# A hybrid scan and expert-retrieval layer on one core: gates built over 64 blocks instead of 48, the projection in six token groups, V loads in another order

## The chip, the cores and the metric

The kernel runs on one core of one Trainium2 chip. The metric is the device time of an execution in microseconds, as the median of several runs; lower is better. Beside it there is one profiled execution, whose span (first to last instruction) and trace are read below.

## What is computed

One layer of a backbone over 1152 tokens (128 prompt tokens and 1024 latent ones) of width 1024: a modulated RMSNorm, an input projection, two kinds of chunked scans, an output projection, and then a product-key expert retrieval (PEER). Cut to the two parts that the change touches:

```python
proj = h @ w_in                          # (t, 1024) @ (1024, 3600)
z, xbc, dt_raw, rq, rk, rv, rg = split(proj)      # 512, 1024, 16, 512, 512, 512, 512
xbc = silu(depthwise_conv(xbc))
...
q = (h @ wq).reshape(t, 8, 2, 128)
s = einsum('thsd,hskd->thsk', q, keys)
s1, i1 = top_k(s[..., 0, :], 16); s2, i2 = top_k(s[..., 1, :], 16)
top, pos = top_k(s1[..., :, None] + s2[..., None, :], 16)
idx = i1 * 128 + i2 of pos; g = softmax(top)
act = gelu(einsum('tkd,td->tk', u_tab[idx], h))   # 128 of 16384 experts per token
y   = einsum('tk,tkd->td', g * act, v_tab[idx])
```

## The kernel before

The stages run one after another: modulation and norm, `project_in` (L291), the scans (`decay_terms`, `chunk_terms`, `mix_tokens`), `score_lists`, `hidden_and_gates` (L1443), `outputs` (L1774). A stage is a block in which every engine has its own stream, and the streams meet only in semaphores. All large products are made from two rounded halves of each operand, so each is three matmuls (`hi hi`, `hi lo`, `lo hi`); `hi` is a copy on ScalarE, `lo` a subtraction on VectorE or GpSimd.

**Projection** (`project_in`). First the 1024 columns of xbc, eight blocks of 128 columns, transposed (columns on partitions, tokens in three chunks of 384), each with a convolution on VectorE and a silu on ScalarE behind it. Then dt: for nine token tiles 24 matmuls of 16 columns each (L423). Then the other 2560 columns as five token groups of 512 columns, each nine tiles of 24 matmuls (L436); ScalarE copies a tile to `st` (L508), SP stores it. GpSimd loads the weights `wt` of group j+2 when group j is done; ScalarE splits them (`split_t`), VectorE makes the rest (`rest_t`, L525). Beside this VectorE makes 64 reductions for the modulation (L568), whose loads SP issues between the stores.

**U stage** (`hidden_and_gates`). The tokens are treated in two ways. Six tiles (768 tokens, TE) are dense: all 16384 experts are computed, as 128 blocks of 128 experts, `s = u h`, each block two halves of 24 matmuls with 384 columns (L1725), gelu on ScalarE (L1523) and a store to `s_d`. ScalarE splits a U block (L1518), GpSimd makes its low part (L1611, `low`) two blocks ahead. Three tiles (GT, 384 tokens) are gathered: GpSimd fetches 384 rows of U (one expert for each of 128 tokens, 512 KB, L1607) into rings of row buffers, and VectorE makes a dot product of each (L1632). In blocks 0 to H1 = 64, VectorE chooses the experts of the nine tiles (`choose`) with 144 (U1) dots between; when that is done it signals `sel_ready`, TensorE turns the lists, ScalarE copies them (`sel_copied`). In the gate blocks (H1 to H2 = 112) the dense gates are built: a group is 8 tokens; VectorE makes two one-hot arrays (L1691), ScalarE scales one by the gates (L1563, `put_gates`), TensorE multiplies them (L1741, `product`), ScalarE copies the result (L1556, `evacuate`) and after every fourth group sends 2 MB to `gates_d`. There are 96 groups, two per block, and 240 dots, five per block. A group needs the product two groups before it. When all dots are there, ScalarE makes their gelu and VectorE adds the first V1 = 48 rows of V.

**V stage** (`outputs`). 128 blocks of 128 experts in periods of BL = 4 blocks, buffers for eight blocks. For each block SP loads `vw` (512 KB) and `ga` (384 KB of `s_d`), and for each period `gt` (1.5 MB of gates). VectorE's `gated(e)` (L1895, 1897, 1899) multiplies by the gates and makes the low parts; ScalarE makes the high parts. TensorE has banks for three token tiles that are `kept` over the whole stage, and two for the other three, which are `taken` once per period: VectorE adds each to `acc` (`take`, L1910). A period on TensorE is taken(j,0), kept(j+1,0), taken(j,1), kept(j+1,1), taken(j,2), kept(j+1,2), kept(j+1,3): 24 matmuls of 512 columns (L1985) for each taken, 18 for each kept. `loads(j+2)` waits until taken(j,2) is done. GpSimd gathers the other VO = 336 rows of V (L1861) into eight buffers, and VectorE adds them (L1882) in `rows_between`, a share after each step of its stream; the shares end in period 27. `finish_first` completes the three gathered tiles, one after each take of period 29.

## Time and profile before

| | us |
|---|---|
| median of 3 runs | 3724.32 (3722.51 to 3728.41) |
| the profiled execution | 3714.26 |
| its span | 3712.6 |
| PE busy | 3380.9 (91%) |
| DVE busy | 2838.1 (76%) |
| POOL busy | 1754.5 (47%) |
| ACT busy | 1253.6 (34%) |
| DMA, mean over the span | 237 GB/s, 880 MB |

PE is TensorE's matmuls, PEld its weight loads, DVE VectorE, ACT ScalarE, POOL GpSimd, SP the engine that issues most loads and stores ("SPq" its queue). "L1725" is a line of the kernel. Times in a timeline are from the start of the span. "x24" is a count; what stands in square brackets at the end of a line is the idle time of the engine just before it and who ended it. PEclk is the granted clock of TensorE as a share of full speed; "DMA share" the mean busy share of the 16 DMA engines (the packets' own times can overlap, so it can pass 1). A matmul's end is modelled, so the pace of matmuls is read from start to start.

### The profile page before, as it was taken

What the parts mean: (1) busy time and instruction counts of PE and PEld (TensorE: products, weight loads), DVE (VectorE), ACT (ScalarE), POOL (GpSimd) and SP (SyncE); (2) the same over time, 40 slices, a digit from 0 to 9 for tenths busy, and PEclk for the clock granted to TensorE, in tenths of its full rate; (3) what the DMA queues carried; (4) which work ended last, traced back from release to release, by engine and by line L of the source; (5) the groups of instructions that cost most, each with busy time, mean ns of one, the idle gap of its engine ahead of it and who ended that gap; (6) DMA issues with size and microseconds to landing.
All of it is one profiled execution on the core that took longest, in us unless ns stands there. A gap on an engine that the chain in (4) does not pass through costs nothing. (4 is left out here: it accounts for less than half of the span.)

```text
span 3712.6 us, 50329 instructions
## 1 busy us (share of the span) xinstructions
PE 3380.9 (91%) x17854; PEld 2992.1 (81%) x17854; DVE 2838.1 (76%) x4693; ACT 1253.6 (34%) x2291; POOL 1754.5 (47%) x1014
## 2 busy tenths in 40 slices
PE   5999969599799999999898899996999999999998
PEld 2998859554799999999888888896777777778786
DVE  4544337497577899999899999954888888888887
ACT  2321125233323222222677777731212212212221
POOL 0000012121111487787788888874655565565530
PEclk8979979799899999999999999998999999999999
DMA  5225424542111578777889898887999999999993
GB/s 183 95 77 168 135 85 156 164 145 85 52 35 47 171 241 270 241 257 250 292 332 342 326 342 343 337 322 279 337 313 343 324 323 332 328 312 336 329 314 122
DMA packets 379343, 880.17 MB, mean 237 GB/s; under 512 B 33554, under 2 KB 192962, under 8 KB 376018
## 3 DMA queue, kind: packets, MB, share of 16 engines
q1 hardware_dynamic: 255876, 390.51, 32.4%
q0 software_dynamic: 116064, 423.24, 31.5%
q10 hardware_dynamic: 7280, 65.01, 4.5%
q8 instruction: 49, 0.80, 0.1%
q14 instruction: 74, 0.61, 0.1%
HBM read 740.54 MB, written 138.11 MB: 237 GB/s over the span
## 5 line engine op out<-in xcount | busy, mean ns | idle before, releaser
L1861 POOL DMA_INDIRECT hT<-peer_v,hT x336 | 571.5, 1701 | 450.9 <-DVE hrow L1882 367.8
L1725 PE MATMUL ps<-h_hi,u_hi 128*128 128x384 f32 x2048 | 699.9, 342 | 30.3 <-POOL u_lo L1611 22.5
L1725 PE MATMUL ps<-h_hi,u_lo 128*128 128x384 f32 x2048 | 690.2, 337 | 0.0
L1725 PE MATMUL ps<-h_lo,u_hi 128*128 128x384 f32 x2048 | 690.1, 337 | 0.0
L1985 PE MATMUL ps<-v_hi,a_hi 128*128 128x512 f32 x1536 | 607.0, 395 | 66.9 <-DVE acc L1910 36.2
L1985 PE MATMUL ps<-vw_rest,a_hi 128*128 128x512 f32 x1536 | 604.4, 393 | 0.0
L1985 PE MATMUL ps<-v_hi,ga_rest 128*128 128x512 f32 x1536 | 603.9, 393 | 0.0
L1607 POOL DMA_INDIRECT hT<-u_rows,hT x224 | 376.6, 1681 | 95.7 <-issue 51.6
L1882 DVE SCALAR_TENSOR_TENSOR hrow<-hT,dots,hrow 128x1024 f32<-128x1024 f32 x336 | 418.1, 1276 | 0.0
L1725 PEld LDWEIGHTS ps<-h_hi,u_hi 128*128 128x128 f32 x2048 | 389.6, 190 | 33.9 <-issue 29.6
L1611 POOL TENSOR_TENSOR u_lo<-uw,u_hi 128x1024 fp32r<-128x1024 f32 x126 | 340.1, 2699 | 157.8 <-ACT u_hi L1518 155.3
L1985 PEld LDWEIGHTS ps<-v_hi,a_hi 128*128 128x128 f32 x1536 | 292.1, 190 | 135.6 <-DVE acc L1910 43.8
L1725 PEld LDWEIGHTS ps<-h_lo,u_hi 128*128 128x128 f32 x2048 | 389.3, 190 | 0.0
L1725 PEld LDWEIGHTS ps<-h_hi,u_lo 128*128 128x128 f32 x2048 | 388.7, 190 | 0.0
L1985 PEld LDWEIGHTS ps<-v_hi,ga_rest 128*128 128x128 f32 x1536 | 292.3, 190 | 61.8
L1985 PEld LDWEIGHTS ps<-vw_rest,a_hi 128*128 128x128 f32 x1536 | 292.7, 191 | 60.9
L1632 DVE CUSTOM_DVE_ANT_0 hT<-hT,hrow 128x1024 f32<-128x1024 f32 x224 | 315.7, 1454 | 32.7 <-DMA hT<-u_rows,hT 31.5
L1523 ACT ACTIVATE so<-ps 128x384 f32<-128x384 f32 x256 | 123.7, 483 | 545.8 <-PE ps L1725 419.8
L1691 DVE TENSOR_TENSOR hT<-iota,sel 128x1024 f32<-128x1024 f32 x192 | 298.0, 1591 | 6.4 <-ACT sel L1546 6.4
L1563 ACT ACTIVATE hT<-hT,sel 128x128 f32<-128x128 f32 x768 | 235.5, 389 | 160.2 <-DVE hT L1691 160.2
L1607 POOL DMA_INDIRECT big<-u_rows,hT x160 | 268.3, 1677 | 43.8 <-issue 40.9
L1839 ACT ACTIVATE a_hi<-ga 128x768 fp32r<-128x768 f32 x128 | 108.5, 848 | 518.2 <-DVE ga L1895 518.2
(338 smaller groups left out, 5889.8 us busy)
## 6 DMA issues: line engine op xcount, KB each, us to landing
uw<-u_T SPq DMA_DIRECT2D x128, 512.0 KB
vw<-peer_v SPq DMA_DIRECT2D x128, 512.0 KB, 11.6
s_d<-so SPq DMA_DIRECT2D x256, 192.0 KB
gates_d<-big ACTq DMA_DIRECT2D x24, 2048.0 KB
gt<-gates_d SPq DMA_DIRECT2D x32, 1536.0 KB
ga<-s_d SPq DMA_DIRECT2D x128, 384.0 KB, 12.1
wmr<-w_modT SPq DMA_DIRECT2D x32, 512.0 KB
tok_d<-st SPq DMA_DIRECT2D x45, 256.0 KB, 2.2
```

The source lines that it names most:

```text
L1523: act.activation(so[b][:], g.ps[4 + 2 * s + b][:, 0:HALF], ACT.Gelu_apprx_tanh).then_inc(act_done, 1)
L1563: z = act.activation(one[s][:, q], one[s][:, q], ACT.Identity, scale=sel3[:, 2, r * G + q:r * G + q + 1])
L1607: pool.indirect_dma_start(rows[slot], None, table, bass.IndirectOffsetOnAxis(ap=g.pick[q][:, i:i + 1], axis=0)).then_inc(row_loaded[slot], 16)
L1611: pool.tensor_tensor(u_lo[e % 2][:], uw[e % 2][:], f(u_hi[e % 2][:]), ALU.subtract).then_inc(u_lo_ready, 1)
L1632: z = dve.tensor_tensor_reduce(rows[slot], rows[slot], g.hrow[:, n // NSEL], 1.0, 0.0, ALU.mult, ALU.add, g.dots[:, n // NSEL, n % NSEL:n ...
L1691: z = dve.tensor_tensor(hot, numbers, sel3[:, i, r * G:(r + 1) * G].unsqueeze(2).broadcast_to([P, G, P]), ALU.is_equal)
L1725: mm = pe.matmul(g.ps[4 + 2 * s + b][:, 0:HALF], u[s][:, k, :], h[:, k, b * HALF:(b + 1) * HALF], start=(k == 0 and i == 0), stop=(k == KD ...
L1839: act.activation(a_hi[s][:], a[s][:], ACT.Copy).then_inc(a_hi_ready, 1)
L1861: pool.indirect_dma_start(rows[n % NU], None, g.v_rows, bass.IndirectOffsetOnAxis(ap=g.pick[m % GT][:, m // GT:m // GT + 1], axis=0)).then ...
L1882: dve.scalar_tensor_tensor(g.hrow[:, q], rows[n % NU], g.dots[:, q, i:i + 1], g.hrow[:, q], ALU.mult, ALU.add).then_inc(added, 1)
L1985: mm = pe.matmul(bank[:], aa[s][:, t * P:(t + 1) * P], v[s][:, q * 512:(q + 1) * 512], start=(start and i == 0), stop=(stop and i == 2), s ...
```

## The change

Three things are changed.

- Projection: dt has no matmuls of its own any more. Its 16 columns stand behind the others, and 16 columns of zeros behind them, in a table `w_tok` of 2592 columns, made on the host; six groups of TW = 432 columns take the place of five of 512. xbc has its own table `w_xbc`. ScalarE copies the first three tiles of the first group ahead of the last silu.
- U stage: the gate blocks are 60 to 123 (64 of them, `PAIRS` = 32 pairs). The first three of the four halves of a pair have a group each. U1 is 128, so 128 dots lie among the lists and 256 in the gate blocks, eight per pair. V1 is 12. ScalarE's loop from H1 on is written out.
- V stage: SP issues the second period's loads only when the second `vw` has landed, and GpSimd its first gather when five blocks are gated. The 372 rows are spread over 29 periods, in shares of 2, 3, 5 and 2 steps; gated() of a period's first block stands behind the five, that of its second behind take(j+1,0), the third and fourth behind take(j+1,1). The three `finish_first` follow one another after the last take of period 29.

```diff
-TC = PROJ - XBC
+TW = 432
+TC = 6 * TW
...
             body(0, 0)
-            with eng.Fori(0, 2) as i:
+            body(1, 1)
+            with eng.Fori(1, NG // 2) as i:
+                body(i * 2, 0)
                 body(i * 2 + 1, 1)
-                body(i * 2 + 2, 0)
...
-            pool.dma_start(wd[:], wv[:, :, 512 + XBC:REST0]).then_inc(wd_loaded, 16)
-            pool.dma_start(wt[0][:], wv[:, :, 0:512]).then_inc(wt_loaded[0], 16)
-            pool.dma_start(wt[1][:], wv[:, :, REST0:REST0 + 512]).then_inc(wt_loaded[1], 16)
+                pool.dma_start(wx[s][:], wv[:, :, s * P:(s + 1) * P]).then_inc(wx_loaded[s], 16)
+            for j in range(2):
+                pool.dma_start(wt[j][:], tv[:, :, j * TW:(j + 1) * TW]).then_inc(wt_loaded[j], 16)
...
-            for j in range(3):
-                pool.wait_ge(group_done, j + 1)
-                c = REST0 + (j + 1) * 512
-                pool.dma_start(wt[j % 2][:], wv[:, :, c:c + 512]).then_inc(wt_loaded[j % 2], 16)
+                    pool.dma_start(wx[s][:], wv[:, :, bass.ds(i * (2 * P) + (2 + s) * P, P)]).then_inc(wx_loaded[s], 16)
+            for j in range(2, NG):
+                pool.wait_ge(group_done, j - 1)
+                pool.dma_start(wt[j % 2][:], tv[:, :, j * TW:(j + 1) * TW]).then_inc(wt_loaded[j % 2], 16)
...
-            pe.wait_ge(wd_lo_ready, 1)
-            for t in range(NT):
-                rows = slice(t * P, (t + 1) * P)
-                for k in range(KD):
-                    for m, (h, w) in enumerate(((h_hi, wd_hi), (h_hi, wd_lo), (g.hT_lo, wd_hi))):
-                        mm = pe.matmul(g.ps[6][:, 16 * t:16 * t + 16], h[:, k, rows], w[:, k, :],
-                                       start=(k == 0 and m == 0), stop=(k == KD - 1 and m == 2))
-            mm.then_inc(dt_done, 1)
-            pe.wait_ge(banks_free, NB + 2)
+            pe.wait_ge(banks_free, NB + 1)
...
-                            mm = pe.matmul(g.ps[t % NQ][:], h[:, k, rows], w[s][:, k, :],
+                            mm = pe.matmul(g.ps[t % NQ][:, 0:TW], h[:, k, rows], w[s][:, k, :],
...
             split_t(1)
+
+            def group(grp, tiles):
+                for t in tiles:
+                    act.wait_ge(tile_done, grp * NT + t + 1)
+                    act.wait_ge(st_stored[t % NQ], grp * (16 * NT // NQ) + (t // NQ) * 16 + 16)
+                    act.activation(st[t % NQ][:], g.ps[t % NQ][:, 0:TW], ACT.Copy).then_inc(tile_copied, 1)
+            group(0, range(NQ))
             silu(NB - 1, 1, NB // 2 - 1)
             act.wait_ge(mod_small, 64)
             act.activation(cb2[:], cb2[:], ACT.Silu).then_inc(mod_silu, 1)
-            act.wait_ge(dt_done, 1)
-            act.activation(dts[:], g.ps[6][:, 0:16 * NT].rearrange("p (t c) -> p t c", t=NT), ACT.Copy).then_inc(dt_copied, 1)
-
-            def group(grp, s):
-                for t in range(NT):
-                    act.wait_ge(tile_done, grp * NT + t + 1)
-                    act.wait_ge(st_stored[t % NQ], grp * (16 * NT // NQ) + (t // NQ) * 16 + 16)
-                    act.activation(st[t % NQ][:], g.ps[t % NQ][:], ACT.Copy).then_inc(tile_copied, 1)
-            for grp in range(5):
-                group(grp, grp % 2)
-                if grp < 3:
+            for grp in range(NG):
+                group(grp, range(NQ if grp == 0 else 0, NT))
+                if grp + 2 < NG:
...
-H1, BODY = 64, 8
-H2 = H1 + DENSE * BODY
+H1 = 60
+H2 = H1 + 64
 NU = 8
 RING1, RING2 = 8, 12
-U1 = 144
+U1 = 128
 LEAD = 8
-V1 = 48
+V1 = 12
...
+            def store_gates(c):
+
+                act.wait_ge(copied, 8 * (c + 1) + 2 * R)
+                act.dma_start(g.gates_d[c].rearrange("p b t -> p (b t)"), out[c % 2]).then_inc(g_stored[c % 2], 16)
...
+            for e in range(H1, NE):
+                for b in range(2):
+                    i = (e - H1) % 2 * 2 + b
+                    if e < H2 and i < THREE:
+                        r = (e - H1) // 2 * THREE + i
+                        evacuate(r)
+                    gelu_half(e, e % 2, b)
+                    if e < H2 and i < THREE and r % 4 == 3:
+                        store_gates(r // 4)
+                if e + 2 < NE:
+                    split_u(e + 2, e % 2, (e + 2) // 2)
+                if e == H2:
+                    act.wait_ge(dots_done, GT * NSEL)
+                    act.activation(g.dots, g.dots, ACT.Gelu_apprx_tanh).then_inc(gelu_done, 1)
...
-            for d in range(DENSE):
-                for k in range(BODY):
-                    e = H1 + d * BODY + k
-                    many = u_rows_by(e) - u_rows_by(e - 1)
-                    group(d * PER + 2 * k)
-                    n = dots(n, many // 2)
-                    group(d * PER + 2 * k + 1)
-                    n = dots(n, many - many // 2)
+            for p in range(PAIRS):
+                many = u_rows_by(H1 + 2 * p + 1) - u_rows_by(H1 + 2 * p - 1)
+                for i in range(THREE):
+                    group(p * THREE + i)
+                    n = dots(n, many * (i + 1) // THREE - many * i // THREE)
...
-            with pe.Fori(0, DENSE) as d:
-                for k in range(BODY):
-                    e, s = d * BODY + (H1 + k), k % 2
+            with pe.Fori(0, PAIRS // 2) as m:
+                for k in range(4):
                     for b in range(2):
-                        product(d, 2 * k + b)
-                        half(e, s, b)
+                        i = k % 2 * 2 + b
+                        if i < THREE:
+                            product(m * (2 * THREE) + (k // 2 * THREE + i), k // 2 * THREE + i)
+                        half(m * 4 + (H1 + k), k % 2, b)
...
-STEPS = 6 + 7 * 28
+SHARE = (2, 3, 5, 2)
+STEPS = sum(SHARE) * 29
...
-            for j in range(2):
-                gates(j, j)
-                loads(j, j)
+            gates(0, 0)
+            loads(0, 0)
+            sp.wait_ge(v_loaded[1], 16)
+            gates(1, 1)
+            loads(1, 1)
...
-            for s in range(RING - 2):
+            for s in range(RING - 3):
                 ready(NE - RING + s, s, NE // RING - 1)
             root(0)
-            for s in range(RING - 2, RING):
+            for s in range(RING - 3, RING):
...
+            pool.wait_ge(a_ready, BL + 1)
...
-            def rows_between(step):
-
-                for n in range(min(VO * step // STEPS, VO), min(VO * (step + 1) // STEPS, VO)):
+            def rows_between(step, many):
+
+                for n in range(min(VO * step // STEPS, VO), min(VO * (step + many) // STEPS, VO)):
                     add_row(n)
-                return step + 1
+                return step + many
...
-            for e in range(BL + 2):
+            for e in range(BL + 1):
                 gated(e)
-                step = rows_between(step)
-            for j in range(NB - 2):
+            for j in range(NB - 1):
                 for t in range(TR):
                     take(j, t)
-                    if j == NB - 3:
-                        finish_first(t)
-                    step = rows_between(step)
-                    for e in ((BL * (j + 1) + 2 + t,) if t < 2 else (BL * (j + 2), BL * (j + 2) + 1)):
-                        gated(e)
-                        step = rows_between(step)
-            dve.sem_inc(ms_ready, 1)
-            for t in range(TR):
-                take(NB - 2, t)
-                if t < 2:
-                    gated(NE - 2 + t)
+                    if j == NB - 3 and t == TR - 1:
+                        for q in range(GT):
+                            finish_first(q)
+                    for e in ((1,), (2, 3), ())[t]:
+                        gated(BL * (j + 1) + e)
+                    step = rows_between(step, SHARE[t])
+                if j < NB - 2:
+                    gated(BL * (j + 2))
+                    step = rows_between(step, SHARE[3])
+                if j == NB - 3:
+                    dve.sem_inc(ms_ready, 1)
...
-        "w_in": A["w_in"][0],
+        "w_xbc": f(A["w_in"][0][:, 512:512 + XBC]),
+        "w_tok": f(np.concatenate([A["w_in"][0][:, 0:512], A["w_in"][0][:, REST0:], A["w_in"][0][:, 512 + XBC:REST0],
+                                   np.zeros((D, TC - (PROJ - XBC)), np.float32)], 1)),
```

## Rows read from the trace of the kernel before

**Rows 1.** Windows: busy us of each engine in two stretches of 100 us (columns named).

```profile
core 0: us, PE busy (x) PEld busy (x) DVE busy (x) ACT busy (x) POOL busy (x), PEclk, DMA share, GB/s
2000.00:2100.00 100.00, 89.77 (x586) 86.80 (x585) 92.03 (x102) 75.11 (x170) 82.53 (x45) 1.00 0.92 346
3000.00:3100.00 100.00, 96.30 (x416) 78.94 (x416) 83.62 (x86) 20.74 (x23) 58.75 (x35) 0.98 0.95 326
```

**Rows 2.** The chain that ended last, V stage: start us, us, what.

```profile
2709.60 7.07 DMA ga<-s_d
...
2743.87 11.73 DMA ga<-s_d
...
3527.25 159.48 PE ps L1985 x702
```

**Rows 3.** Matmuls of the projection by line: min/median/max ns, first and last start us.

```profile
L423 PE MATMUL ps<-wdt_hi,pi_h_hi x72: 171/361/362, 196.7 to 238.2; 128*128 128x16 f32 x72
...
L436 PE MATMUL ps<-wt_hi,pi_h_hi x360: 388/394/774, 238.8 to 490.0; 128*128 128x512 f32 x180
```

**Rows 4.** Timeline before the token groups, ACT, then DVE: start us, us, instruction.

```profile
194.67 3.61 ACT L458 ACTIVATE wt_hi<-wt 128x4096 fp32r<-128x4096 f32 x1
...
198.31 4.42 DVE L525 TENSOR_TENSOR wt_rest<-wt,wt_hi 128x4096 fp32r<-128x4096 f32 x1 [3.22 <-ACT wt_hi L458]
```

**Rows 5.** Timeline of ACT, first halves of two plain blocks of U.

```profile
2505.57 0.49 ACT L1523 ACTIVATE so<-ps 128x384 f32<-128x384 f32 x1 [3.57 <-PE ps L1725]
...
2513.89 0.49 ACT L1523 ACTIVATE so<-ps 128x384 f32<-128x384 f32 x1 [3.58 <-PE ps L1725]
```

**Rows 6.** Timeline where the gate blocks begin, DVE, then ACT.

```profile
1762.16 1.21 DVE L1632 CUSTOM_DVE_ANT_0 hT<-hT,hrow 128x1024 f32<-128x1024 f32 x1
1763.31 0.07 DVE L1632 DVE_READ_ACCUMULATOR2_ANT dots<- 128x1 f32 x1
...
1768.41 0.50 DVE L1679 COPY hT<-big 128x128 f32<-128x128 f32 x3
...
1771.58 0.49 ACT L1523 ACTIVATE so<-ps 128x384 f32<-128x384 f32 x1 [3.67 <-PE ps L1725]
...
1794.26 0.47 ACT L1523 ACTIVATE so<-ps 128x384 f32<-128x384 f32 x1
```

**Rows 7.** Groups of instructions by form in the gate blocks, 1850 to 2400 us.

```profile
L1691 DVE TENSOR_TENSOR hT<-iota,sel 128x1024 f32<-128x1024 f32 x163 | 257.4, 1618 | 0.0
L1607 POOL DMA_INDIRECT big<-u_rows,hT x133 | 226.4, 1702 | 36.4 <-issue 34.3
...
L1632 DVE CUSTOM_DVE_ANT_0 big<-big,hrow 128x1024 f32<-128x1024 f32 x135 | 178.5, 1349 | 21.3 <-DMA big<-u_rows,hT 21.1
...
L1611 POOL TENSOR_TENSOR u_lo<-uw,u_hi 128x1024 fp32r<-128x1024 f32 x41 | 112.5, 2745 | 40.2 <-ACT u_hi L1518 39.9
```

**Rows 8.** Timeline of gate blocks: a product on PE, then first halves on ACT.

```profile
1934.16 2.05 PE L1741 MATMUL ps<-hT 128*128 128x128 f32 x16
...
2427.32 0.53 ACT L1523 ACTIVATE so<-ps 128x384 f32<-128x384 f32 x1
```

**Rows 9.** Timeline at the start of the V stage, SP queue and PE.

```profile
2568.35 9.43 SPq L1814 DMA_DIRECT2D vw<-peer_v  x1
...
2594.43 0.77 PE L1985 MATMUL ps<-v_hi,a_hi 128*128 128x512 f32 x1 [30.65 <-DVE ga_rest L1899]
```

**Rows 10.** One V period on DVE, then a stall on PE: timeline.

```profile
3309.10 0.96 DVE L1895 TENSOR_TENSOR ga<-ga,gt 128x768 f32<-128x768 f32 x1 [6.98 <-DMA ga<-s_d]
...
3311.98 2.47 DVE L1882 SCALAR_TENSOR_TENSOR hrow<-hT,dots,hrow 128x1024 f32<-128x1024 f32 x2
...
3005.89 0.50 PE L1985 MATMUL ps<-v_hi,a_hi 128*128 128x512 f32 x1 [2.95 <-DVE acc L1910]
```

**Rows 11.** Row gathers of the V stage by line: first and last start us.

```profile
L1861 POOL DMA_INDIRECT hT<-peer_v,hT x336: 939/1696/4626, 2568.6 to 3569.4; - x168
```

**Rows 12.** Window of 10 us near the start of the V stage; columns as in rows 1.

```profile
2610.00:2620.00 10.00, 10.00 (x46) 8.29 (x45) 10.00 (x12) 3.60 (x4) 8.69 (x4) 1.00 1.04 394
```

More of the change, by code:

```diff
@@ L299, in project_in @@
     NQ = 3
+    NG = TC // TW
     with ExitStack() as ctx:
@@ L431, in group @@
                     rows = slice(t * P, (t + 1) * P)
-                    if not (isinstance(grp, int) and t < NQ):
+                    if not (isinstance(grp, int) and grp * NT + t < NQ):
                         pe.wait_ge(tile_copied, grp * NT + (t - NQ + 1))
@@ L1566, in _ @@
             put_gates(1, 1)
-            for d in range(DENSE):
-                for k in range(BODY):
-                    e, s = d * BODY + (H1 + k), k % 2
-                    for b in range(2):
-                        q = 2 * k + b
-                        evacuate(d, q)
-                        if d * PER + q + R < TE // G:
-                            put_gates(d * PER + q + R, q % R)
-                        gelu_half(e, s, b)
-                    split_u(e + 2, s, d * (BODY // 2) + (H1 + k) // 2 + 1)
-                    if k % 2 == 1:
-                        act.wait_ge(copied, d * (2 * PER) + 4 * (k + 1) + 2 * R)
-                        act.dma_start(g.gates_d[bass.ds(d * 4 + k // 2, 1)].rearrange("o p b t -> p (o b t)"), out[k // 2 % 2]).then_inc(g_stored[k // 2 % 2], 16)
-            plain(H2, 0, H2 // 2)
-            act.wait_ge(dots_done, GT * NSEL)
-            act.activation(g.dots, g.dots, ACT.Gelu_apprx_tanh).then_inc(gelu_done, 1)
-            plain(H2 + 1, 1, H2 // 2)
-            with act.Fori(H2 // 2 + 1, NE // 2 - 1) as j:
-                plain(j * 2, 0, j)
-                plain(j * 2 + 1, 1, j)
-            gelu(NE - 2, 0)
-            gelu(NE - 1, 1)
+            for e in range(H1, NE):
[12 more added lines that the diff above has]
+                    act.activation(g.dots, g.dots, ACT.Gelu_apprx_tanh).then_inc(gelu_done, 1)
             for s in range(2):
@@ L1731, in hidden, with product @@
                 half(e, s, 1, first)
-            def product(d, q):
-                r = d * PER + q
+            def product(r, q):
                 pe.wait_ge(hot_ready, r * 2 + 2)
```

54 lines of the change are left out of this document (20 added, 34 removed).

## Prediction

> **What bounds the kernel now.** I read the windows by stage first, then the chain that ended last, then for each stage the group or the timeline that shows which wait ends last. The profiled execution spans 3712.6 us (3714.26 us with what lies around it); the median of the runs shown is 3724.32, so 10 us above it. I sum against 3714.26 and add the 10 at the end. Three stages are touched. (1) The projection: TensorE is busy without a break, but part of that is 216 tiny matmuls for dt [rows 3]. (2) The U stage (128 blocks of 48 matmuls): a plain block takes 8.32 us, from first half to first half [rows 5]. In the 48 gate blocks VectorE is 92% busy, TensorE 90%, GpSimd 83% and the DMA engines 92% [rows 1]; from the first half of block 64 (1794.26) to that of block 111 (2427.32) it is 47 blocks in 633 us, 13.5 each [rows 6, 8]. (3) The V stage: TensorE 96%, DMA 95%, VectorE 84% [rows 1]; the chain goes in turn through a load landing, VectorE, TensorE [rows 2]. So here the order of VectorE's work against the landing decides, with the DMA engines close behind.
>
> **Projection, part by part.** Removed: 216 dt matmuls, which run from 196.7 to 238.8 [rows 3]: 42.1 us on TensorE with nothing beside them that needs the time. Added: 16 columns of dt and 16 of padding in the token groups. Before: 45 tiles of 24 matmuls with 512 columns in 251 us (238.8 to 490.0), 5.58 per tile, 232 ns per matmul; the plain pace is 227 ns at 512 columns (159.48 us / 702, [rows 2]) and 8.32 us / 48 = 173 ns at 384 [rows 5]. Between them, 432 columns give 193 ns, 54 tiles x 24 x 193 = 250.5 us; with six group ends instead of five and the slow first matmuls (774 ns against a median of 394, [rows 3]) I take 255, so +4. The dt matmuls also covered the split of the first weights: with them gone TensorE waits from 196.7 until wt_lo is there. Today ScalarE takes 3.61 us and VectorE then 4.42, until 202.7 [rows 4]; at 432/512 of that, and without the wdt split ahead, 201.2, so +4.5. Sum: -42.1 + 4 + 4.5 = **-34** (bounds -38 if the start costs nothing more, -28 if each group end waits 1 us for its weights or a store). ScalarE takes the first three tiles ahead of the last silu, so the fourth tile finds its bank free, and each later load of weights has most of a group's 42 us to land and be split.
>
> **Where the gate blocks begin.** VectorE finishes the lists and the gates at about 1768.9 (the copies that start at 1768.41, [rows 6]), TensorE the last half of block 63 at 1771.6, when ScalarE takes it. The two are level now. The change takes away four blocks (33.3 us) from TensorE but only 16 dots from VectorE, at 1.15 us (1762.16 to 1763.31, [rows 6]): 18.4 us. So TensorE will wait for sel_ready, and the gate blocks begin 18.4 us, not 33 us, earlier (bounds -15 and -22: the row gathers hold low parts of U a little more or less). The transposes and the first product cost the same as now: first half of block 64 at 1794.26 [rows 6], of block 60 then at 1776, before the 34 of the projection are taken off.
>
> **The gate blocks.** Per two blocks now: VectorE 8 comparisons x 1.618 + 10 dots x 1.349 = 26.4 us, GpSimd 2 x 2.745 + 10 gathers x (1.702 + 0.27 of issue) = 25.2 and a 2 us wait for u_hi [rows 7], TensorE 2 x 8.32 + 4 products of 1.8 = 23.8 (a product of 16 passes shows 2.05 with its modelled end [rows 8]; start to start it is 1.8). Measured 2 x 13.5 = 27, so VectorE and GpSimd set it. After: six comparisons and eight dots, 20.5 us on VectorE; 5.5 + 8 x 1.97 = 21.3 on GpSimd; 16.6 + 3 x 1.8 = 22.0 on TensorE, which becomes the bound. With three engines within 1.5 us of one another I don't take 22.0 but 23.2 (end points 22.0, and 25.0 if two of the waits stay as they are). 32 pairs x 23.2 = 742 us, to 2518; four plain blocks and the last two halves, 33 us, to 2551. The stage ends now at 2567.9, just ahead of the first issue of the next one [rows 9]. So the U stage gives **-17** with its start included (bounds -55 with pairs of 22.0, +41 with pairs of 25.0). The store of gates, 24 of 2 MB as before, and the wait for the gelu of the dots with 12 V rows behind it (12 x 1.3 = 16 us on VectorE) are hidden by the last three blocks (25 us).
>
> **The V stage.** 36 rows move here: 336 gathers from 2568.6 to 3569.4 now [rows 11], 372 after, spread over 29 periods instead of 28.
> - Start. TensorE begins at 2594.43, 26.5 us after the first load; the first weight load is stuck behind gt for 9.43 us in SP's queue [rows 9], while 8 row gathers and the second gt share the engines. With both held back, gt, one vw and one ga are 2.5 MB; at 394 GB/s [rows 12] 6.3 us, plus issue and landing and VectorE's 2.9, some 15 us: **-11** (bounds -5 and -15).
> - Periods. 144 matmuls at 227 ns are 32.7 us of TensorE. From the first kept blocks (2611) to the last row it is 28 periods in 974 us, 34.8 each. The 2.1 us are lost so: loads(j+2) are issued when taken(j,2) is done, land 7.1 to 11.7 us later [rows 2], and VectorE, which goes straight into gated() of the first two of these blocks, stands still (6.98 us in [rows 10]) and is then late for take(j+1,0), so TensorE waits 2.95 us for acc [rows 10]. The new order puts five row additions (1.2 us each, [rows 10]: 2.47 for two) ahead of one gated() (2.9 us) and the other gated() behind take(j+1,0): 9.4 + 2.9 + 2 rows x 1.2 + 0.6 = 15.3 us after taken(j,2), where TensorE wants take(j+1,0) after 17.7 us (kept 4.1 + 4.1, taken 5.4, kept 4.1). By this the stall is gone. Against it stands DMA: a period moves 5.24 MB of blocks and 12.8 rows of 0.52 MB, 11.97 MB against 11.53 now; at 32.7 us that is 366 GB/s, where the stage runs at 326 with the engines 95% busy [rows 1]. 10 us at 394 GB/s are seen [rows 12], so 366 is not out of reach, but not with loads that come in bursts. I take 34.7 us (345 GB/s, the value of [rows 1] for the gate blocks, 346). 29 x 34.7 = 1006, against 28 x 34.8 + 32.7 = 1007: **-1** (bounds 33.2 and 36.5 per period: -44 and +51).
> - End. The three finish_first now stand in one lump (some 11 us of VectorE) ahead of gated(124): TensorE reaches it after 13.6 us, VectorE after 14 or 15: **+3**.
>
> The Trainium skill, "DMA: Bandwidth & Descriptors", section Bandwidth, gives about 358 GB/s as a core's share of HBM, and 425 for a core alone. By 358 the period would be 33.4 us and the change worth 38 us more; the trace shows 394 for 10 us, above the share, and no long stretch above 346, so neither figure bounds the sum.
>
> **Sum**: -34 - 17 - 11 - 1 + 3 = -60; 3714.3 - 60 = 3654 for a profiled run, **3664 us** for the median.
>
> **Rivals.**
> - Forecast, 3664 us: chance 0.55.
> - V stage at TensorE's pace: nothing but the order held it, period 33.2. 29 x 1.5 = 43 less, 3621. For it: the stall row and its releaser. Against: 95% DMA. Chance 0.15.
> - V stage DMA-bound at today's rate: 11.97 MB at 331 GB/s (11.53 MB in 34.8) is 36.1 us; 29 x 1.4 = 41 more: 3705. For it: the engines 95% busy, and five gathers in a burst. Against: the stage loses that share partly in the stall. Chance 0.19.
> - Gate blocks stay late: GpSimd's gathers and low parts run into each other, 25.0 per pair, 32 x 1.8 = 58 more: 3722, no change that can be told (0.2% is 7 us, about what this measurement can tell). Chance 0.05.
> - Slower: the five row additions free five buffers just when loads(j+2) are issued, so five gathers compete with the first vw and ga. A row takes 1.5 us of all engines at 346 GB/s; three more than now ahead of the loads add 4.5 us, and equal shares with the rest of gt 2 more: landing at 16 instead of 9.4. Then gated() ends at 18.9, 5.3 us after TensorE wants it (13.6), and every period is 38: 29 x 3.3 = 96 more, 3760. It turns to slower than before once landings exceed 14.8 us (period 36.8). Against: the queue holds at most eight rows at any time now too. Chance 0.06.
>
> The Trainium skill, the same page, section Queues, rings and completion order, says that an engine takes turns between the queues it has work for, packet by packet. By this rule the loads would get about half of the engines while rows are queued, which is that last rival; 9.43 us for an issue behind gt [rows 9] speak for it, and no row shows the shares themselves.
>
> **Range**: 3622 to 3712 leaves out the slow rivals and half of the fastest one. Faster by over 0.2% 0.89, within 0.2% 0.05, slower 0.06.
>
> **What the profile would show.** No matmul of 16 columns, the token groups beginning near 201 and ending near 457. Block 60's half waiting for sel_ready, with VectorE the releaser. Gate pairs of 23.2 us, TensorE over 94% and VectorE under 92% busy. In V: first matmul 15 us after the stage begins, DVE's wait for ga short, no acc releaser on TensorE, DMA share 0.97 or more, period 34.7. The forecast fails if a gate pair takes 25 us, or if landing takes over 15 us in V.

## The result and the profile after

| | before | after |
|---|---|---|
| median, 4 runs each on one chip | 3725.64 us (3722.51 to 3728.41) | 3615.95 us (3615.19 to 3617.31) |
| ratio, 95% interval | | 0.9706 [0.9691, 0.9722] |
| span of the profiled execution | 3712.6 us | 3613.5 us |

The change saves 110 us where 60 were forecast, and the time lies below the range. Between the two profiled executions it is 99.1 us. Most of the other 11 are the distance of before's profiled execution from its own median: the runs of before lie between 3712 and 3733 us in all comparisons below, those of after within 2.1 us of one another.

By stage, worked out from the first and last instructions in the two traces (us):

| | before | after | change | forecast |
|---|---|---|---|---|
| start to the first U matmul | 1201.7 | 1180.3 | -21.4 | -34 |
| first U matmul to the first load of gt, where V begins | 1366.2 | 1351.4 | -14.9 | -17 |
| load of gt to the first V matmul | 26.5 | 15.9 | -10.6 | -11 |
| V matmuls, first to last (periods and end) | 1102.8 | 1050.6 | -52.2 | -1 + 3 |
| last V matmul to the end | 15.4 | 15.3 | 0 | 0 |

The V matmuls took 54 us less than forecast and the projection 13 us more; the other rows come within 2 us, the U stage by luck, as shown below. Windows of after, columns as in [rows 1]; two stretches of gate blocks, two of V:

```profile
2000.00:2100.00 100.00, 95.09 (x610) 94.08 (x609) 81.62 (x91) 68.37 (x147) 77.76 (x43) 0.98 0.88 320
2100.00:2200.00 100.00, 92.21 (x586) 90.90 (x586) 83.14 (x95) 68.57 (x153) 77.44 (x43) 0.98 0.88 320
3000.00:3100.00 100.00, 100.00 (x443) 82.84 (x442) 93.54 (x95) 21.93 (x24) 60.22 (x39) 1.00 1.00 365
3100.00:3200.00 100.00, 100.00 (x443) 82.84 (x442) 93.06 (x94) 21.91 (x24) 56.06 (x40) 1.00 1.02 370
```

In V TensorE has no gap left, where [rows 1] has 96%. VectorE is at 93%, since it adds more rows in a shorter time, and the DMA engines move 365 to 370 GB/s where it was 326. The chain that ended last says it in one row (start us, us, what):

```profile
2532.10 5.87 SPq L1792
2538.02 6.45 DMA ga<-s_d
...
2547.60 989.66 PE ps L1965 x4356
```

4356 of the 4608 matmuls follow one another without a wait, at 227.2 ns; 4608 of them are 1046.9 us, and they take 1050.6. In [rows 2] the chain came back to a landing of 7 to 12 us. The waits of VectorE in the V stage follow (total us, times, longest). The first pair of rows is before from 2600 to 3600; the second is after from 2560 to 3530, where these two rows are all there are:

```profile
DVE ga L1895 <- DMA ga<-s_d: 140.4, 36, 7.3
...
DVE acc L1910 <- PE ps L1985: 13.5, 10, 1.8
```

```profile
DVE acc L1891 <- PE ps L1965: 59.9, 35, 2.2
DVE acc L1888 <- PE ps L1965: 12.0, 4, 7.1
```

No wait for a load is left; VectorE waits for TensorE. A piece of one period of VectorE in after's timeline:

```profile
3016.67 1.28 DVE L1891 TENSOR_TENSOR acc<-acc,ps 128x512 f32<-128x512 f32 x2
3017.86 6.16 DVE L1863 SCALAR_TENSOR_TENSOR hrow<-hT,dots,hrow 128x1024 f32<-128x1024 f32 x5
3023.94 0.94 DVE L1876 TENSOR_TENSOR ga<-ga,gt 128x768 f32<-128x768 f32 x1
```

The next loads are issued when TensorE has done the bank that the first line of this piece adds to acc. VectorE adds five rows of V, 6.2 us, and then finds ga landed: there is no idle time in front of the third line, where [rows 10] has 6.98 us.

Part of the 52 us is TensorE's clock, which the forecast did not look at. The clock is granted at one of two levels, 1.2 or 2.4 GHz (PEclk 0.5 or 1.0). Behind the stall of 2.95 us in [rows 10] it stood at the lower one:

```profile
3007.00:3010.00 3.00, 3.00 (x8) 2.35 (x8) 3.00 (x4) 1.47 (x2) 2.69 (x2) 0.50 1.09 369
```

Matmuls start 0.43 us apart there (3006.69 to 3009.67) instead of 0.227. Over the V stage of before, 104 matmuls start 240 to 520 ns after the one ahead of them, together 18 us above the plain pace; in after it is 11, for 2 us. So about 16 of the 52 us are the lower clock that came with the stalls, and the rest is the stalls themselves.

### The profile page after: what moved, and what is told of

The parts are those of the page before. It is cut to its first block and busy times, and to the rows that moved or that the text cites. A ratio compares the mean times of both kernels' runs of the same rounds, so it can differ in the third digit from the quotient of the medians.

```text
span 3613.5 us, 50302 instructions
## 1 busy us (share of the span) xinstructions
PE 3330.6 (92%) x17854; PEld 2994.0 (83%) x17854; DVE 2813.8 (78%) x4693; ACT 1252.5 (35%) x2299; POOL 1653.7 (46%) x1014
## 5 line engine op out<-in xcount | busy, mean ns | idle before, releaser
L1842 POOL DMA_INDIRECT hT<-peer_v,hT x372 | 547.2, 1471 | 444.7 <-DVE hrow L1863 329.4
L1965 PE MATMUL ps<-v_hi,a_hi 128*128 128x512 f32 x1536 | 598.7, 390 | 22.9 <-DVE ga_rest L1880 20.4
L1863 DVE SCALAR_TENSOR_TENSOR hrow<-hT,dots,hrow 128x1024 f32<-128x1024 f32 x372 | 457.3, 1285 | 0.0
L1587 POOL DMA_INDIRECT hT<-u_rows,hT x212 | 342.6, 1616 | 120.5 <-DVE dots L1612 71.0
L1612 DVE CUSTOM_DVE_ANT_0 hT<-hT,hrow 128x1024 f32<-128x1024 f32 x212 | 296.4, 1441 | 60.0 <-DMA hT<-u_rows,hT 58.8
L1612 DVE CUSTOM_DVE_ANT_0 big<-big,hrow 128x1024 f32<-128x1024 f32 x172 | 225.1, 1339 | 100.1 <-DMA big<-u_rows,hT 100.0
L1587 POOL DMA_INDIRECT big<-u_rows,hT x172 | 276.8, 1609 | 46.5 <-issue 43.9
```

The lines of the kernel that those rows point to most:

```text
L1587: pool.indirect_dma_start(rows[slot], None, table, bass.IndirectOffsetOnAxis(ap=g.pick[q][:, i:i + 1], axis=0)).then_inc(row_loaded[slot], 16)
L1612: z = dve.tensor_tensor_reduce(rows[slot], rows[slot], g.hrow[:, n // NSEL], 1.0, 0.0, ALU.mult, ALU.add, g.dots[:, n // NSEL, n % NSEL:n ...
L1842: pool.indirect_dma_start(rows[n % NU], None, g.v_rows, bass.IndirectOffsetOnAxis(ap=g.pick[m % GT][:, m // GT:m // GT + 1], axis=0)).then ...
L1863: dve.scalar_tensor_tensor(g.hrow[:, q], rows[n % NU], g.dots[:, q, i:i + 1], g.hrow[:, q], ALU.mult, ALU.add).then_inc(added, 1)
L1965: mm = pe.matmul(bank[:], aa[s][:, t * P:(t + 1) * P], v[s][:, q * 512:(q + 1) * 512], start=(start and i == 0), stop=(stop and i == 2), s ...
```

## The experiments

The kernel before was run beside each group of them on the same chip; its medians were 3720.73, 3721.07 and 3719.86 us. All ratios are to these.

### Is V short by its own order, or by what comes before it?

**v_only** is before with the new V stage alone (336 rows in it); **v_old** is after with the whole V stage of before (372 rows).

```diff
 v_only: before, with outputs() and STEPS of after
 v_old:  after, with outputs() and STEPS of before
```

> The kernel of before with nothing changed but the V stage (new order and start; 336 rows as before). The order theory: TensorE's pace of 32.6 us per period, stage 1082 us as in the changed kernel, since rows are not what bounds it: 3725.6 - 63 = 3663 us. The rival, that 36 fewer rows in the U stage or the new gate blocks are needed for the gain: 3700 us or more.

> The changed kernel with the whole V stage of before (order of gated, takes and row additions, loads, start), but with the 372 rows. The order theory: VectorE stands still at the first ga of a period as before and has 36 rows more to add at 1.2 us, so the V stage (first gt issue to the end) takes 1144.7 + 43 = 1188 us instead of 1082, and the kernel 3722 us. The rival, that the V stage got shorter because of the U stage's end or the gates and not of its own order: V stage 1145 at most, 3680 us or less.

v_only took 3653.83 us (3648.03 to 3657.28), ratio 0.9824 [0.9804, 0.9844], near the 3663 of the theory of the order and far from the rival's 3700; v_old 3665.55 us (3650.94 to 3671.17), 0.9845 [0.9813, 0.9877]. From the load of gt to the end v_only needs 1081.8 us, as after does, against 1144.7 in before. Its windows show TensorE full:

```profile
2700.00:2800.00 100.00, 100.00 (x443) 82.81 (x442) 89.01 (x91) 21.90 (x24) 48.12 (x36) 1.00 0.95 344
3000.00:3100.00 100.00, 100.00 (x443) 82.81 (x442) 88.94 (x90) 22.04 (x24) 47.58 (x35) 1.00 0.96 350
```

So the gain of V belongs to the V stage alone, and a DMA share of 0.95 goes with a full TensorE, while the same share went with 96% in [rows 1]: the share alone did not tell whether the loads were the bound. v_old was 56 us faster than its expectation by the theory of the order (3722), which had 36 more rows lengthen every period. The V matmuls did not get longer: 1090.7 us in v_old against 1102.8 in before, with the DMA engines at 350 GB/s:

```profile
3100.00:3200.00 100.00, 96.21 (x424) 79.00 (x422) 88.10 (x90) 22.58 (x24) 63.32 (x38) 1.00 0.97 350
```

The reading that fits is that VectorE adds the extra rows in time in which it waited for ga: without the one long wait at the start of the stage it waits 102 us in v_old and 146 in before (134.5 - 32.4 and 182.3 - 36.2), and 36 rows at 1.2 us are 43. Why V then took 12 us less is open: V in the old order took 1102.8, 1111.5 and 1116.3 us in three kernels with identical V stages.

### The order undone, the rest left

**v_gated_first** is after with one thing put back: gated() of the next period's first block comes ahead of the five row additions. Rows, shares and start are those of after.

```diff
+                    if t == TR - 1 and j < NB - 2:
+                        gated(BL * (j + 2))
                     step = rows_between(step, SHARE[t])
                 if j < NB - 2:
-                    gated(BL * (j + 2))
                     step = rows_between(step, SHARE[3])
```

> The changed kernel with gated() of the next period's first block ahead of the five row additions instead of behind them. If the five rows that fill the landing time are what removed the stall: 9.4 + 2.9 + 7 x 1.2 + 0.6 = 21.3 us after taken(j,2), where TensorE wants take at 17.7, so 3.6 us per period and more with slow matmuls behind it: 3616 + 29 x 4 = 3732 us. The rival, that it is enough to have one gated() instead of two ahead of the take: 3616 to 3630 us.

Measured: 3709.21 us (3705.49 to 3715.8), ratio 0.9969 [0.9957, 0.9981]. The V matmuls take 1145.3 us, 94.7 more than in after, 3.3 a period. The same three instructions in its timeline, in the other order, and the wait that it makes; then the waits from 2560 to 3640 and two windows:

```profile
3124.84 1.28 DVE L1891 TENSOR_TENSOR acc<-acc,ps 128x512 f32<-128x512 f32 x2
3130.37 0.96 DVE L1876 TENSOR_TENSOR ga<-ga,gt 128x768 f32<-128x768 f32 x1 [4.25 <-DMA ga<-s_d]
...
3133.26 7.36 DVE L1863 SCALAR_TENSOR_TENSOR hrow<-hT,dots,hrow 128x1024 f32<-128x1024 f32 x6
```

```profile
DVE ga L1876 <- DMA ga<-s_d: 140.0, 29, 6.7
...
PE ps L1966 <- DVE acc L1891: 63.7, 29, 4.6
```

```profile
3000.00:3100.00 100.00, 96.87 (x417) 79.39 (x418) 85.89 (x89) 22.25 (x24) 58.12 (x34) 0.98 0.94 341
3100.00:3200.00 100.00, 90.77 (x379) 73.79 (x378) 87.08 (x88) 19.27 (x21) 51.02 (x39) 0.95 0.87 314
```

This is the cause, moved by hand: one instruction group in another place costs 93 us, and the rival (one gated() less ahead of the take is enough, 3616 to 3630) is out. The 93 us are the price of this place in the new schedule. They are not what before lost: after with the whole old V stage (v_old) is only 50 us slower than after, so v_gated_first is worse than the old order, and it waits more for ga (4.8 us a period, v_old 3.5). Why the old order waits less was not looked into. A ledger of VectorE gives the size of the 93. In after it is busy 827 of the 880 us from 2620 to 3500, 30.7 us of a period of 32.7. If it also waits 140.0 / 29 = 4.8 us in each, it needs 35.5, and TensorE must follow; the period measured is 36.0. The clock has a share in that: here 145 matmuls start 240 to 520 ns after the one ahead, together 25 us above the plain pace, so some 23 of the 94.7 us are the lower clock. Without the wait 30.7 is less than 32.7, and TensorE sets the pace. In before it is busy 843.5 us and waits 140.4 of the 1000 from 2600 to 3600, together 98% of the time: there too the two fill it.

### How much room did the DMA engines have?

**dma1** and **dma3** are after with one or three copies of 512 KB from HBM to HBM in each V period, which nothing waits for.

```diff
                     loads(m * 2 + i, i)
+                    for c in range(3):    # dma1: range(1)
+                        sp.dma_start(g.dump[...], g.u_rows[...]).then_inc(dumped, 16)
```

> The changed kernel with one more transfer per period of the V stage, 512 KB from one place in HBM to another, which nothing waits for until the end. At TensorE's pace the stage then moves 12.5 MB per period, 382 GB/s. The theory that DMA has no room left at 366 GB/s (engines at 1.00): periods of 12.5 / 366 = 34.2 us, 29 x 1.5 = 44 more, 3660 us. The order theory with room left up to the 394 GB/s seen for 10 us: 3616 to 3622 us.

> The kernel after with three more copies of 512 KB from HBM to HBM in each V period, which nothing else waits for: at 32.7 us a period that asks for 414 GB/s, where one copy (381 GB/s) cost nothing. If the ceiling of the DMA engines lies near the 394 GB/s of the window of the prediction, the period becomes 34.3 us and 29 x 1.6 = 46 us come on top: about 3662. If it lies at 381, the period is 35.5 us: about 3698. If 414 can still be had: 3616 to 3622.

dma1 took 3619.38 us (3617.9 to 3620.87), ratio 0.9724 [0.9709, 0.9739], with 1050.2 us of V matmuls; dma3 3716.14 us (3711.07 to 3729.99), ratio 0.9996 [0.9984, 1.0008], with 1151.4. Two windows of dma1, then one of dma3, and a piece of dma3's chain:

```profile
2700.00:2800.00 100.00, 100.00 (x443) 82.81 (x442) 94.69 (x96) 22.38 (x25) 58.94 (x42) 1.00 1.05 386
3000.00:3100.00 100.00, 100.00 (x443) 82.80 (x442) 93.53 (x95) 21.92 (x24) 58.24 (x40) 1.00 1.04 381
```

```profile
2800.00:3000.00 200.00, 189.58 (x826) 155.83 (x825) 173.96 (x175) 42.20 (x46) 109.64 (x73) 0.98 1.01 378
```

```profile
3088.80 17.58 DMA ga<-s_d
3109.51 53.82 PE ps L1968 x228
...
3165.19 10.89 DMA ga<-s_d
```

381 to 386 GB/s can be had without a matmul being late. With three copies, which ask for 414, the landings in the chain are 9 to 18 us, VectorE waits for ga again (89.7 us in 15 times from 2700 to 3600), and the period is 36.0 us (1050.6 + 100.8, the 100.8 spread over 30 periods), in which 13.54 MB move, 376 GB/s. That is worse than each of the three expectations; 3698 was the nearest. The rate alone would have given 13.54 / 0.386 = 35.1 us. Of the 100.8 us about 20 are matmuls at the lower clock (125 of them, counted as above, 22 us against 2 in after). What else makes up the rest, the rate of such copies or the burst in which they stand in the queue, wasn't separated, so 376 is no ceiling. For after it is enough: it asks for 366 GB/s and had 15 to 20 more.

The Trainium skill, "DMA: Bandwidth & Descriptors", section Bandwidth, has about 358 GB/s as a core's share when both cores of a pair stream, and 425 for a core alone. The traces agree in that a core alone moved 365 to 386 GB/s, above the share, in windows of 100 us; no run here reached 425, and where 414 was asked for, 376 came.

### The start of V by itself

**v_old_start** is after with the second gt and the row gathers no longer held back.

```diff
-            gates(0, 0)
-            loads(0, 0)
-            sp.wait_ge(v_loaded[1], 16)
-            gates(1, 1)
-            loads(1, 1)
+            for j in range(2):
+                gates(j, j)
+                loads(j, j)
...
-            pool.wait_ge(a_ready, BL + 1)
```

> The changed kernel with the old start of the V stage (both periods' loads at once, gathers at once). If the start is worth what the traces show, first matmul 26.5 us after the first issue instead of 16, and as the rest runs at TensorE's pace nothing of it is caught up: 3626.5 us. The rival, that the start is made up later: 3616 us. Its row shares begin at take(0,0) in either case.

Measured: 3630.04 us (3629.13 to 3630.97), ratio 0.9756 [0.9737, 0.9775]. The first V matmul comes 27.2 us after gt instead of 15.9, and the first weight load is stuck for 10.64 us again, where after has 5.87:

```profile
2534.47 10.64 SPq L1792 DMA_DIRECT2D vw<-peer_v  x1
```

The start is worth 11 us as forecast; the whole run is 14 us slower than after.

### The projection by itself

**proj_only** is before with the new project_in() and the weights laid out for it; **store_first** is after with each load of the modulation's weights issued four tiles later, behind the stores of the tiles.

```diff
 store_first:
-                    if 2 <= grp * NT + t < 4 * KD:
-                        load_mod(grp * NT + t)
                     sp.wait_ge(tile_copied, grp * NT + t + 1)
                     sp.dma_start(g.tok_d[...], st[t % NQ][:]).then_inc(st_stored[t % NQ], 16)
+                    if 2 <= grp * NT + t - 4 < 4 * KD:
+                        load_mod(grp * NT + t - 4)
```

> The kernel of before with the new projection alone. If the stages are independent, it gives what the two traces show up to the first matmul of U (1201.7 against 1180.3): 21 us less, 3699 us. My forecast of 34 us would give 3687 us. A rival, that the later stages answer to the shift: any other value, up to 3721.

> The changed kernel; in the projection SP stores a tile first and issues the modulation load of four tiles earlier after it, so that a store never waits behind a load that waits for VectorE. If the 12 us that TensorE stands still in the token groups come from that queue (st waits for a store, the store stands behind load_mod), the groups take 253 us instead of 264.6 and the kernel 3606 us. The rival, that they come from the first wait for weights and the group ends: 3616 us.

proj_only took 3696.85 us (3695.25 to 3701.38), ratio 0.9935 [0.9921, 0.9949]: 24 us, near the 21 of the two traces and not the 34 of the forecast. Its first U matmul is at 1174.6, 27 us earlier than in before. store_first took 3617.89 us (3614.96 to 3619.71), 0.9723 [0.9708, 0.9738]: nothing, as the rival had it. The token matmuls of after by line, TensorE's waits in 190 to 470 us, and ScalarE's wait for a free store buffer, in after and then in store_first:

```profile
L423 PE MATMUL ps<-wt_hi,pi_h_hi x432: 352/358/698, 204.0 to 468.2; 128*128 128x432 f32 x144
...
PE ps L423 <- ACT st L488: 4.8, 3, 3.5
PE ps L423 <- DVE wt_rest L509: 4.6, 1, 4.6
...
ACT st L488 <- DMA tok_d<-st: 61.3, 15, 9.8
```

```profile
ACT st L488 <- DMA tok_d<-st: 6.1, 1, 6.1
```

The groups take 264.6 us in after (before: 251.7) and 263.4 in store_first. ScalarE's 55 us of waiting for the store's queue vanish and TensorE gains 1 us. So hardly any of that wait reached TensorE, which has three banks between itself and ScalarE.

### Why a pair of gate blocks takes 24 us, not 22

The pairs of after are bound by no engine: in the windows at the top TensorE has 92 to 95%, VectorE 82%, GpSimd 78%. The pairs are not alike either. From the first matmul of a pair to that of the next, 15 pairs of after, from block 74 on, go 26.0, 23.7, 23.8, 22.0, 26.5, 23.0, 23.9, 22.0, 26.7, 22.8, 23.8, 22.0, 26.8, 22.8, 23.8 us: one in four is long, and one in four has the 22.0 that the work of TensorE adds up to. VectorE's waits from 1750 to 2300 follow, and one place in the timelines of VectorE, ScalarE and GpSimd, each in order of time:

```profile
DVE big L1612 <- DMA big<-u_rows,hT: 64.9, 30, 6.3
DVE hT L1612 <- DMA hT<-u_rows,hT: 36.2, 17, 7.0
```

```profile
1837.51 1.23 DVE L1612 CUSTOM_DVE_ANT_0 big<-big,hrow 128x1024 f32<-128x1024 f32 x1 [6.16 <-DMA big<-u_rows,hT]
...
1844.37 2.35 DVE L1671 TENSOR_TENSOR hT<-iota,sel 128x1024 f32<-128x1024 f32 x2
...
1848.93 4.56 DVE L1671 TENSOR_TENSOR hT<-iota,sel 128x1024 f32<-128x1024 f32 x2
...
1839.91 2.44 ACT L1551 ACTIVATE hT<-hT,sel 128x128 f32<-128x128 f32 x8 [7.11 <-DVE hT L1671]
...
1833.72 0.94 POOL L1587 DMA_INDIRECT big<-u_rows,hT  x1 [0.30 <-issue]
1834.68 2.36 POOL L1591 TENSOR_TENSOR u_lo<-uw,u_hi 128x1024 fp32r<-128x1024 f32 x1
...
1842.13 1.98 POOL L1587 DMA_INDIRECT big<-u_rows,hT  x1 [0.30 <-issue]
1849.49 2.92 POOL L1591 TENSOR_TENSOR u_lo<-uw,u_hi 128x1024 fp32r<-128x1024 f32 x1 [5.38 <-ACT u_hi L1499]
```

It reads as a ring: VectorE's dot waits for a row, ScalarE waits for the comparisons queued behind that dot on VectorE, GpSimd waits for u_hi behind that on ScalarE, and the gathers of the next rows are queued behind GpSimd's low part. What the ring turns on is how many gathers run ahead of the dots, LEAD. So LEAD was changed alone: **lead10** and **lead9** on after, **before_lead10** on before.

```diff
-LEAD = 8
+LEAD = 10
```

> The changed kernel with LEAD 10 instead of 8 (U rows are gathered two rows further ahead). If late rows set the gate pairs of 23.9 us (VectorE waits 101 us for rows between 1750 and 2300), the wait shrinks and pairs come down to 22.5 to 23.2: 3616 - 32 x 1 = 3584 us, 3593 at least. The rival, that GpSimd then waits for free buffers ahead of the low part of U, so that TensorE waits for u_lo: 3625 us or more.

> The kernel after with lead 9 instead of 8 (10 gave 3559.3 us, 8 gives 3616). If the lead works gradually, row by row (each row of lead is one gather, 1.97 us, earlier than the dot product that waits for it), half of the gain is here: 3583 to 3592. If it works by a threshold (one more row is enough to open the ring of waits, since the waits of VectorE are 1 to 7 us each and a gather is about 2), nearly all: 3560 to 3570.

> The kernel before with only the lead of the U row gathers at 10 instead of 8. Theory: with 48 gate blocks VectorE itself is the bound (26.4 us of work in a pair of 27.0 us), and its waits for rows are 39.7 us in the 600 us from 1800 on; a longer lead can give back those waits at most, 10 to 15 us in what TensorE sees: 3706 to 3718 beside 3721. Rival: the lead is worth as much here as in the kernel after (57 us), since the ring of waits between the three engines is there in both: 3665 to 3680. No third: if this kernel doesn't move at all, the waits of before were hidden.

| | median, us | ratio, 95% interval | first to last product, us | a pair, us |
|---|---|---|---|---|
| after | 3615.95 | 0.9706 [0.9691, 0.9722] | 753.4 | 23.9 |
| lead9 | 3573.71 (3568.27 to 3577.86) | 0.9603 [0.9585, 0.9620] | 715.2 | 22.7 |
| lead10 | 3559.29 (3555.73 to 3561.98) | 0.9562 [0.9548, 0.9577] | 699.1 | 22.2 |
| before_lead10 | 3696.64 (3684.66 to 3697.93) | 0.9928 [0.9905, 0.9951] | 624.0 | 26.3 |

(A pair is two gate blocks; from first to last product there are 63 blocks, in before_lead10 47.5, where before takes 647.0 us, 27.2 a pair.) lead10 did better than its expectation, 3584 to 3593. lead9 (3574) lies between its two, 3583 to 3592 and 3560 to 3570: three quarters of the gain come with the first row of lead, so it is neither in proportion nor a plain threshold. Windows of lead10 and of lead9, one of before_lead10 with GpSimd's groups in it, and the waits of VectorE in lead10 from 1750 to 2300:

```profile
2000.00:2100.00 100.00, 100.00 (x659) 100.00 (x658) 93.61 (x101) 74.79 (x167) 87.82 (x46) 1.00 0.96 351
```

```profile
2000.00:2100.00 100.00, 98.26 (x641) 97.95 (x641) 88.54 (x100) 75.88 (x168) 81.48 (x44) 1.00 0.90 332
```

```profile
1850.00:2350.00 500.00, 471.32 (x3054) 460.73 (x3053) 449.09 (x535) 399.20 (x885) 447.22 (x230) 0.99 0.95 352
...
L1607 POOL DMA_INDIRECT big<-u_rows,hT x128 | 233.9, 1827 | 35.2 <-issue 33.7
L1607 POOL DMA_INDIRECT hT<-u_rows,hT x63 | 116.4, 1847 | 17.2 <-issue 15.9 <-DVE dots L1632 0.6
L1611 POOL TENSOR_TENSOR u_lo<-uw,u_hi 128x1024 fp32r<-128x1024 f32 x39 | 97.7, 2505 | 0.7
```

```profile
DVE hT L1671 <- PE ps L1717: 24.0, 18, 1.5
DVE big L1612 <- DMA big<-u_rows,hT: 9.8, 6, 3.1
DVE hT L1612 <- DMA hT<-u_rows,hT: 1.1, 3, 0.5
```

The wait for rows falls from 101 us to 11, TensorE is full, and a pair comes to 22.2, where the prediction's sum of TensorE's work was 22.0; from matmul to matmul 30 of the 32 pairs take 22.0. The same step on before is worth 23 us, more than the 3 to 15 that were expected and far from 57. A pair comes to 26.3 there, but VectorE is not what holds it, which the expectation had taken for granted: it is busy 449 of the 500 us from 1850 to 2350 and waits 51 for rows. GpSimd is the one without a break: busy 447 us, 50 more between its instructions that go to issue, 0.7 waiting for u_hi. With ten gathers in a pair its work is the floor, with eight it is not. That shows what the 64 blocks are for. The U stage went from 1366.2 to 1351.4 us with lead 8, but from 1340.1 to 1298.2 with lead 10: 15 us against 42.

### The three finish_first

**lead10_spread** is lead10 with one finish_first after each take of period 29.

```diff
-                    if j == NB - 3 and t == TR - 1:
-                        for q in range(GT):
-                            finish_first(q)
                     for e in ((1,), (2, 3), ())[t]:
                         gated(BL * (j + 1) + e)
+                    if j == NB - 3:
+                        finish_first(t)
```

> The kernel after with the lead of the U row gathers at 10 instead of 8, and besides the three finish_first one after each take of period 29 instead of all three after its last take. In the run with lead 10 alone (3559.3 us) VectorE works on the three from 3481.33 to 3493.11, and TensorE then waits 2.4 us for acc and 1.2 us for ga_rest. If the lump is what costs that, as the prediction had it with +3, this run comes to 3555 to 3556 us. Rival: the waits only move to the last two periods, where VectorE and TensorE take turns in any case: 3559.

Measured: 3562.95 us (3560.62 to 3568.88), ratio 0.9584 [0.9567, 0.9601]: not faster. TensorE waits 3.6 us for acc in place of the lump's 2.4, because the first finish_first now waits for its own data:

```profile
DVE hrow L1904 <- DMA hT<-x_d: 7.9, 1, 7.9
...
PE ps L1964 <- DVE acc L1891: 3.6, 1, 3.6
```

The lump gives the load of x time to land. It costs after 3.7 us (1050.6 - 1046.9), and spreading it brings nothing.

lead10 is the best version: 3559.3 us, 4.4% under before and 57 us under after.

## Why the prediction was wrong

- **V periods: the step that failed.** "I take 34.7 us (345 GB/s ...)", -1 us; measured 32.7 us. The stage's matmuls came 52 us earlier to their end, and with the 3.7 of the end taken out the periods gave 56. The half of the argument that was a mechanism held: the prediction counted 15.3 us on VectorE against the 17.7 that TensorE leaves, and wrote "by this the stall is gone". Then it took a rate in place of that conclusion, the highest that a long stretch of before had shown. But 326 and 346 GB/s were what the stages asked for at their pace, not what the engines could give: v_only asks for less and has a full TensorE at 0.95 share; dma1 moves 386. The row of 394 GB/s [rows 12] was the right witness, and was set aside as too short. The rival "V at TensorE's pace" (0.15) is what happened, and its 33.2 was itself too careful. That its 3621 lies within 5 us of the measured 3616 is partly luck: it had 11 us too little in V and 13 too much in the projection, and the 10 us that the prediction added for the median did not come, since the runs of after lie within 2 us.
- **The clock: left out.** The prediction gave all 2.1 us that a period of before lost to VectorE's lateness. [rows 1] had 0.98 as granted clock there. 18 of the 56 us that the V stage of before takes over the plain pace are matmuls at the lower clock behind the stalls, so the prize for the stall was stalls and clock together.
- **The slower rival** (five gathers crowd the loads) didn't come: the loads land within the five rows. The place it named is real, though. v_gated_first shows 3.3 us a period as soon as VectorE meets the landing, and dma3 shows landings of 10 to 17 us when something does crowd them.
- **Projection: mis-sized, -21.4 for -34.** The dt matmuls went as forecast (42.3 us), and the start gap is 5.0 for 4.5. The groups cost 12.9 more for +4: 54 tiles of 4.68 us are 252.7, 195 ns a matmul for the 193 assumed, and 11.9 us are the rest, where 4.5 had been put. The x part ended 2.5 us later in this execution, which is spread: over the ten traces with the new projection and the rest of after, the first U matmul comes between 1175.5 and 1181.3. The bound of -28 was too narrow. Of the 11.9 us, 4.8 are waits for ScalarE, 1.6 are at group ends, and about 3 are the lower clock, in 6.4 us of two stretches behind the gap at the start and a wait of 3.5 us at 237; the last 2 to 3 us are open, and SP's queue is not it (store_first).
- **Where the gate blocks begin: mis-sized, right engine.** The first product comes 24.8 us earlier after the first U matmul, for -18.4 and a bound of -22. VectorE is ready 24.7 us earlier, so it does set the start, but a dot there isn't 1.15 us. That price was the distance of two that stood back to back; the group of before's dots from 1300 to 1760 us has a mean of 1514 ns with next to no idle time before them, and 16 x 1.514 is 24.2. The mean is a mixture: some 110 of the 133 take 1.2 us and the others 2.0 to 3.4. So the match is a reading and not shown, as four blocks less are also four low parts less beside VectorE. The row of the group:

```profile
L1632 DVE CUSTOM_DVE_ANT_0 hT<-hT,hrow 128x1024 f32<-128x1024 f32 x133 | 194.2, 1514 | 1.0
```

- **The gate pair: 23.9 for 23.2.** The forecast had the three engines "within 1.5 us of one another" and put 1.2 us on it for that. The cost is there and is 1.9 (1.7 if pairs are counted from first matmul to first matmul, 758.6 us for 32); by lead10, where those pairs take 22.0, it is wait for rows and not the engines' work.
- **The sum of the U stage: right by luck,** -14.9 for -17. The start came 6.4 us earlier than forecast and the pairs took 16 more (758.6 for 742). The rest is a wrong anchor: 1794.26 in [rows 6] is ScalarE taking the first half of block 64, 11.7 us after that half's first matmul (1782.60); in a plain block it takes a half 4.5 us after its first matmul. The 742 us were so counted from some 7 us too late.
- **Start of V: right,** -10.6 for -11, shown by v_old_start. **End: right,** 3.7 for 3.

## What to carry to other kernels

- A DMA rate read in a stage that waits for something else is what the stage asked for. Before a rate is taken as a bound, look for the fastest window of the trace, or add a copy that nobody waits for and see whether anything gets later.
- Add up the work of an in-order engine and its waits for landings in a period, and compare the sum with the pace of the engine that should set it. When work alone fits and work with waits doesn't, other work put between issue and use gives back the whole wait: with five row additions behind the use and not ahead of it, this kernel is 93 us slower.
- Count a stall of TensorE with the granted clock behind it: here a stall of 3 us was followed by some 3 us of matmuls at 1.2 GHz, and that was a third of what the stage lost.
- An average per period can hide a pattern. Look at each period before giving all of them the same cost.
- Where no engine is full in a stage, look for a ring of waits, and try the number that says how far the producer runs ahead. The gain ends at the next engine's own work, so add that up too.

## What the runs showed of the hardware

- One core kept 365 to 386 GB/s of mixed loads, stores and row gathers for hundreds of us, with the DMA share at 1.00 to 1.05. A share of 0.95 went once with a full TensorE and once with a starved one.
- TensorE's granted clock fell to 1.2 GHz in or right behind stalls of 1.8 to 3.8 us in the V stage of before, most often for about 3.3 us: eight times behind its start, and never in after between 2560 and 3590, where TensorE has no stall.
- VectorE's comparison of 128x1024 takes either 1.2 us or 3.4 us, and nothing between: of those that start from 1850 to 2350 us, 21 of 125 take 3.4 in after and 40 of 136 in lead10. The 4.56 us of two at 1848.93 above are one of each, and the long one stands beside GpSimd's low part (1849.49, 2.92 us), about as if VectorE had stood still meanwhile:

```profile
L1671 DVE TENSOR_TENSOR hT<-iota,sel x2: 1218/2322/3426, 1848.9 to 1850.1; 128x1024 f32<-128x1024 f32 x2
```

- A gather's issue takes 0.94 us while VectorE waits (1833.72) and 1.98 while it works (1842.13). It reads as if a VectorE that waits less made the gathers slower: from 1800 to 2400 their mean is 1620 ns in after and 1668 in lead10. The comparison's mean, 1593 and 1847, moves with the number of long ones.
